# Four weighted one-hot rows of eight on ScalarE in place of three, in a hybrid decoder step

## The reference

```
q = (xb @ w_q).reshape(blk, PEER_HEADS, 2, PEER_DKH)
sc = jnp.einsum('nhpd,hpkd->nhpk', q, sub_keys)
sv, si = lax.top_k(sc, PEER_TOPK)
cand = sv[..., 0, :, None] + sv[..., 1, None, :]       # 16 x 16 sums per head
cidx = si[..., 0, :, None] * N_KEYS + si[..., 1, None, :]
fv, fi = lax.top_k(cand, PEER_TOPK)
eidx = take_along_axis(cidx, fi); gate = softmax(fv)
act = gelu(einsum('nd,nhed->nhe', xb, u_tab[eidx]))
y = einsum('nhe,nhed->nd', gate * act, v_tab[eidx])
```

## Time and profile before

| what | value |
|---|---|
| median of 3 runs | 3357.64 us |
| profiled execution | 3359.98 us |
| its span | 3358.1 us |
| granted clock of PE, mean | 0.971 |
| PE busy | 3180.1 us, 95% |
| DVE busy | 2682.0 us, 80% |
| ACT busy | 1399.6 us, 42% |

### The profile page before, as it was taken

The page is one execution under the profiler, slowest core; times in us unless marked ns, Lnnn a source line. Parts: engine busy times, 40 slices in busy tenths (PEclk is TensorE's granted clock), DMA queues, the critical chain, the costliest instruction groups (busy, mean ns, idle before and its releaser), DMA issues.

```text
span 3358.1 us, 48956 instructions
## 1 busy us (share of the span) xinstructions
PE 3180.1 (95%) x18217; PEld 2897.1 (86%) x18217; DVE 2682.0 (80%) x5395; ACT 1399.6 (42%) x2317; POOL 1188.0 (35%) x766
## 2 busy tenths in 40 slices
PE   8899998998999999999989989899989999999999
PEld 7788897998888888888879578889988888888888
DVE  6546389888688888888868937998878888888887
ACT  4553214777333333333333232277843333333332
POOL 2122320000455455555542033100025555555554
PEclk9887999999999999999999989999999999999999
DMA  3121222554999999999952322245579999999997
GB/s 126 50 63 59 90 70 89 204 205 145 377 375 369 358 370 358 362 367 359 368 166 65 13 82 70 71 160 206 204 266 381 363 371 358 367 358 363 368 358 268
DMA packets 425212, 807.82 MB, mean 241 GB/s; under 512 B 234176, under 2 KB 259328, under 8 KB 421504
## 3 DMA queue, kind: packets, MB, share of 16 engines
q1 hardware_dynamic: 318496, 453.12, 40.1%
q0 software_dynamic: 94560, 344.45, 27.6%
q10 hardware_dynamic: 11920, 7.12, 1.4%
HBM read 729.52 MB, written 76.08 MB: 240 GB/s over the span
## 4 chain that ended last, share of the span: by engine, by line
PE 77%; DVE 17%; ACT 3%; DMA 2%; issue 1%; POOL 0%; SPq 0%; ACTq 0%; DVEq 0%
PE bank L921 31%; PE bank L909 27%; PE bank L662 11%; DVE cv L2082 4%; PE bank L892 3%; DVE oh L1727 1%; DVE oh L1722 1%; DMA units_ahead<-ga 1%; DVE eidx L1606 1%; PE bank L804 1%; PE bank L849 1%; PE bank L649 1%; DVE ring L1736 1%; DVE pick L1599 1%; PE bank L820 1%
## 5 line engine op out<-in xcount | busy, mean ns | idle before, releaser
L909 PE MATMUL bank<-hh,ring 128*128 128x384 f32 x4096 | 1094.8, 340 | 36.8 <-DVE sc L1557 20.5
L921 PE MATMUL bank<-ring,wh 128*128 128x512 f32 x3072 | 828.4, 391 | 0.6 <-DVE wl L1754 0.6
L2139 POOL DMA_INDIRECT rows<-in_utab,gidx x320 | 450.5, 1408 | 1041.9 <-ACT stage L1213 608.9
L1736 DVE TENSOR_TENSOR ring<-raw,ring 128x1024 fp32r<-128x1024 f32 x506 | 616.5, 1221 | 240.4 <-ACT ring L1081 239.5
L909 PEld LDWEIGHTS bank<-hh,ring 128*128 128x128 f32 x4096 | 748.0, 189 | 45.7 <-issue 37.8
L1081 ACT ACTIVATE ring<-raw 128x1024 fp32r<-128x1024 f32 x598 | 622.0, 1052 | 212.1 <-PE bank L909 94.0
L909 PE MATMUL bank<-hl,ring 128*128 128x384 f32 x2048 | 689.4, 337 | 0.0
L921 PEld LDWEIGHTS bank<-ring,wh 128*128 128x128 f32 x3072 | 574.4, 188 | 112.0 <-DVE ring L1736 0.8
L2139 POOL DMA_INDIRECT rows<-in_vtab,gidx x320 | 492.4, 1539 | 367.1 <-DVE acc L1776 314.3
L662 PE MATMUL bank<-hh,ring 128*128 128x272 f32 x2752 | 494.6, 298 | 55.0 <-DVE hl L1511 48.2
L1175 ACT ACTIVATE ga<-bank 128x384 f32<-128x384 f32 x256 | 124.7, 487 | 986.0 <-PE bank L909 969.2
(11 more groups left out here) (318 smaller groups left out, 2870.3 us busy)
## 6 DMA issues: line engine op xcount, KB each, us to landing
raw<-in_stream SPq DMA_DIRECT2D x342, 512.0 KB, 5.7
raw<-in_vtab SPq DMA_DIRECT2D x256, 512.0 KB, 8.0
gate_matrix<-stage SPq DMA_DIRECT2D x24, 2048.0 KB, 11.5
gt<-gate_matrix SPq DMA_DIRECT2D x256, 192.0 KB, 9.6
units_ahead<-ga SPq DMA_DIRECT2D x96, 192.0 KB, 4.4
gv<-units_ahead SPq DMA_DIRECT2D x96, 192.0 KB, 8.7
rows<-in_utab,gidx POOLq DMA_INDIRECT x320, 8.1
rows<-in_vtab,gidx POOLq DMA_INDIRECT x320, 7.8
```

The source lines that it names most:

```text
L909: m = T.matmul(PB[1][:, (e + 1) % 2, 0:ND], w[:, ring_slot(t), k * P:(k + 1) * P], h[:, k, 0:ND], start=(k == 0 and i == 0), stop=(k == KC ...
L921: m = T.matmul(psum[c][:, a, :], w[:, v_n % WSLOT, c * P:(c + 1) * P], v[:, ring_slot(t), 512 * a:512 * a + 512], start=(v_n == 0 and i == ...
L1736: V.tensor_tensor(ring_lo[:, ring_slot(t), :], raw[raw_buffer(t)][:], ring_hi[:, ring_slot(t), :].bitcast(F32), ALU.subtract).then_inc(s_l ...
L2139: nc.gpsimd.indirect_dma_start(out=rows[:, g % ROW_SLOTS, :], out_offset=None, in_=vtab if is_v else utab, in_offset=bass.IndirectOffsetOn ...
```

## The change

`ACT_OH` goes from 3 to 4: ACT makes the weighted rows of tokens 0 to 3 of each group, DVE those of tokens 4 to 7. The buffer of the distances grows from three to four rows of 128 and is allocated in the other zone, behind the last raw-tile buffer.

```
-ACT_OH = 3
+ACT_OH = 4
...
             slT = sb("slT", [P, 2, 4, P], F32, z)
-            dist = sb("dist", [P, ACT_OH, P], F32, z)
...
             raw_more = [sb(f"raw{i}", [P, D], F32, z) for i in range(2, 4)]
+            dist = sb("dist", [P, ACT_OH, P], F32, z)
```

## The result

The changed kernel takes 3383.28 us (median of 4 runs, 3382.4 to 3383.53), the kernel before 3356.95 (4 runs): a ratio of 1.0078, 95% interval 1.0063 to 1.0093. It is slower by 26 us where 20 were forecast (3378 us). The profiled execution took 3383.32 us, its span 3381.5.

The account below looks back on a forecast made before the run. ACT was taken to become the fuller engine in the gate stretches, ending last at some groups; 9.0 us a layer, 18 in two, plus 2 for PE's clock gave 3380 on the profiled execution, so 3378 us, range 3364 to 3392.

Parts of the forecast that it names:

- What bounds the stretch: While the gate matrix is built, ACT becomes fuller than DVE (about 250 against 238 us); "issue" waits are for ACT's rows.
- Prices: Fourth row costs ACT 0.68 us per group, 65 us in all, and takes 25 us from DVE.
- The move of the buffer: The distances' buffer gets another address with the same writer, reader and order: priced at zero.
- Halves 2, 4, 5 and 6: Of a layer's six eight-group halves, these shift by +2.8, +2.6, +3.4 and -1.5 us: groups 8-15, 24-31, 32-39, 40-47.
- Group 47's wait for DVE: The last group of a layer still hangs on DVE, and its 4.33 us wait gets shorter; half 6 gains 1.5 us.
- Halves 1 and 3: Groups 0 to 7 and 16 to 23 of each layer: +0.6 and +1.1 us, through ACT's delayed rows and gelus.
- PE's clock: Longer waits may lower PE's clock; one more dip than before, 2 us, bounds -4 to +14.
- The sum: Halves add 9.0 us a layer, 18 in two, plus 2 for the clock: 3378 us, slower by 0.6%.
- VectorE as the bound that hides ACT's part: In the gate stretches ACT's added time costs nothing: 6 us won, 3352 us, or up to 25, 3333; chance 0.07.
- the change is absorbed: Pairs lie beside PE's unit tiles and gains offset the rest: within 7 us of before, about 3360; chance 0.08.
- ACT might be exposed everywhere: Nothing covers ACT's pairs: 65 us, 3423; with half covered, 3390 to 3400; chance 0.05.
- The rival of the clock: PE's clock drops with each new wait: the forecast's 18 plus 14 us, 3390; chance 0.10.

Follow-up runs that it names:

- the second experiment: Kernel before, with ACT also making a fourth pair into a spare row while DVE keeps its five rows: 3390.68 us, ratio 1.0094.
- the complement kernel: Kernel before, with four rows on ACT only for groups 0 to 8, 17 to 24 and 41 to 47, three elsewhere: 3363.06 us, ratio 1.0017.
- the filler: Changed kernel plus fourteen useless matmuls on PE ahead of the second tile after groups 7 and 23: 3376.69 us, ratio 1.0059 to the kernel before.
- the third experiment: Kernel before, with DVE making four rows, ACT still three, and PE multiplying the third row twice: 3351.3 us, ratio 0.9977.

## Why the prediction was right, and what was mis-sized

*What bounds the stretch.* Right. The wait named "issue" was ACT's pair, as group 31 had suggested; the second experiment shows it with DVE's rows unchanged.

*Prices.* Right: 0.68 us per pair (2.86 us on the median from the pair's start to the instruction behind it, 2.18 before) and 65 and 25 us in all.

*The move of the buffer.* Right: nothing.

*Halves 2, 4, 5 and 6.* Right to within 0.2 us, but for half 2 of layer 1, in which the clock fell. In half 4 of layer 0 the single steps agree too: groups 27, 29 and 31 are late by 1.35, 1.91 and 2.53 us, where 1.36, 1.9 and 2.6 had been worked out. With the three tiles after each half PE starts the next one afresh, so the halves could be summed; the write of the stage is what still reaches across. Group 47's wait for DVE went as worked out; it answers to the earlier trace rows:

```profile
831.57 2.80 PE L892 MATMUL bank<-oh 128*128 128x128 f32 x16 [3.92 <-issue]
...
842.02 2.05 PE L892 MATMUL bank<-oh 128*128 128x128 f32 x16 [0.87 <-DVE oh L1727]
```

*Halves 1 and 3.* Right in the chain: the complement kernel shows group 19 late by 0.44 us, where 0.4 had been worked out, and from group 22 to the second tile after 23 the way is 0.68 us longer, as worked out. Two things were left out in half 3. The write of the stage, which is queued behind ACT's pair, cost 0.6 us in layer 0 and nothing in layer 1. And between groups 19 and 22 PE won back 0.3 us of the delay. Without the slow clock half 3 comes to 1.4 us in layer 0 and 0.6 in layer 1, on either side of the 1.1; half 1 comes to 0.6 and 0.4, where 0.6 stood.

*PE's clock.* This term was mis-sized: 2 us were taken and about 9 are seen in the five places, of which the filler gave back 7 in four. I had priced a dip by group 45's alone (1.5 us) and counted one more than before. The waits for the gelu in halves 1 and 3 grew to 2.3 to 3.4 us, and the clock fell in all four. Of half 1's I had expected no dip at all.

*The sum.* The halves gave 26.2 us where 18 + 2 stood. Without the clock's 9 that is 17. That the medians differ by 26.3 as well is in part chance: the profiled run of before lay 3.0 us above its median (3359.98 against 3356.95), and the two profiled spans differ by only 23.4. Of the halves' sum 2.8 us came back elsewhere, 2.0 of it between the last group of layer 0 and the first of layer 1. The largest piece there, 1.7 us, is the sums of the norm behind layer 0, before and after:

```profile
1729.42 9.29 PE L649 MATMUL bank<-hf_conv,con 128*128 128x272 f32 x32 [1.90 <-DVE xt L1825]
```

```profile
1742.44 7.60 PE L649 MATMUL bank<-hf_conv,con 128*128 128x272 f32 x32 [1.91 <-DVE xt L1825]
```

That is not the change's doing. Among the ten profiles of this study these sums took 7.60 us in six and 9.29 in four, in kernels that are the same there and after the same wait. The granted clock over them is 1.00 in the six and 0.82 in the four, so this too is the clock.

*Rivals.* VectorE as the bound that hides ACT's part falls with the third experiment: its relief alone is worth 7.5 us, close to the 6 that were worked out for it, but ACT's cost stands beside it and is four times as large. The Trainium skill's advice (Perfetto Trace Analysis, "Optimizing Scalar/DVE Operations") is that offloading work to Scalar may make sense when DVE is saturated. Here DVE was the busier engine over the stretch (88%), but it ended last only at some groups, and one row more on ACT at every group lost 26 us; the table with counts of 1 to 5 shows that it can pay where the count follows the group. That the change is absorbed falls by its 26 us. That ACT might be exposed everywhere falls too: 32 us of 65 came out. The rival of the clock is half true: with about 9 us the clock cost more than the 2 that were taken and less than that rival's 14, since it fell after some of the new waits and not after others.

## What to carry to other kernels

When two engines make parts of one operand, the busier one over a stretch need not be the one that the consumer waits for: look at each place for the engine that ends last, and for what stands behind it in its queue (here copies, gelus and a write). A fixed split lost in both directions, +7 and +26 us, while a split chosen per group from the trace of before won 20 us with the same total work. A new idle time of PE can also cost through the clock afterwards, which here was about a third of the loss (9 of 26 us).

## What the runs showed of the hardware that was not expected

After waits of about the same length PE's clock falls in one execution and not in another. Group 15 in half 2 of layer 1 took 3.19 us after 2.14 us of waiting, and group 31, after 2.14, took 2.02. Before the change, group 45 took 3.50 us after 3.19 and 2.05 after 3.17. The norm's sums, after 1.9 us of waiting each time, ran at 0.82 in four executions and at 1.00 in six. What such a fall costs can be read from the rows; whether it comes could not be told from them here, and what decides it stays open. At the four places ahead of two full tiles the clock fell each time, and 3 us of filler matmuls on PE were enough for 1.00 in each.
